# Conditioning blocks moved between the quarters of x, first recurrent block summed chunk by chunk, and a reciprocal root by exp and ln

## What is computed

```python
ada = (silu(c) @ w_ada + b_ada)                 # 6 vectors of 2048: shift1, scale1, gate1, shift2, scale2, gate2
h = rmsnorm(x, g_pre1) * (1.0 + scale1) + shift1
z = h @ w_in                                    # columns: pool | LRU | pool gate | LRU gate
y_pool = pool_mix(u_pool)                       # trailing means, per-group map
xc = causal_dwconv(u_lru)                       # width 4
r, i = sigmoid(xc @ w_rg + b_rg), sigmoid(xc @ w_ig + b_ig)     # 8 diagonal blocks of 256
a = exp(-8 * r * softplus(-lam)); u = sqrt(1 - a**2) * (i * xc)
h_t = a_t * h_{t-1} + u_t                       # the recurrence
x = x + gate1 * rmsnorm((sigmoid(g_pool) * up(y_pool) + sigmoid(g_lru) * up(y_lru)) @ w_out, g_post1)
x = x + gate2 * rmsnorm(conv_ffn(rmsnorm(x, g_pre2) * (1 + scale2) + shift2), g_post2)
```

## Time and profile before

| | |
|---|---|
| median of 3 runs | 2651.7 us (2651.51 to 2810.54) |
| the profiled execution, its own time | 2655.3 us |
| its span on the slowest core | 2653.8 us (cores: 2639.4 to 2653.8) |
| PE busy | 2256.0 us (85%) |
| DVE busy | 1186.9 us (45%) |
| ACT busy | 851.8 us (32%) |
| POOL busy | 146.6 us (6%) |
| mean granted TensorE clock of that core | 0.933 |
| mean DMA rate | 128 GB/s |

### The profile page before, as it was taken

The page is one execution under the profiler, slowest core; times in us unless marked ns, Lnnn a source line. Parts: engine busy times, 40 slices in busy tenths (PEclk is TensorE's granted clock), DMA queues, the critical chain, the costliest instruction groups (busy, mean ns, idle before and its releaser), DMA issues.

```text
span 2653.8 us, 42396 instructions; the slowest of 8 cores (2639.4 to 2653.8 us)
## 1 busy us (share of the span) xinstructions
PE 2256.0 (85%) x16896; PEld 1147.8 (43%) x16896; DVE 1186.9 (45%) x2346; ACT 851.8 (32%) x1111; POOL 146.6 (6%) x281
## 2 busy tenths in 40 slices
PE   2215888887899999997688888999999999999993
PEld 0012444443455555553344444445554545555551
DVE  1842787996511111122445555643003775663005
ACT  2142787885200000011233344432002434442000
POOL 0000000000000000000000000000000000000000
PEclk9557999998899999998898999999999999999996
DMA  9485755464243544466658877778776997778961
GB/s 247 133 134 89 139 108 99 91 116 93 48 88 73 102 89 80 80 120 131 165 96 164 176 138 135 133 143 168 133 130 116 198 186 136 135 135 159 200 126 72
DMA packets 61970, 338.45 MB, mean 128 GB/s; under 512 B 7504, under 2 KB 8016, under 8 KB 28240
## 3 DMA queue, kind: packets, MB, share of 16 engines
q0 software_dynamic: 39888, 273.17, 57.4%
q1 hardware_dynamic: 21888, 62.56, 7.1%
HBM read 586.69 MB, written 22.17 MB: 229 GB/s over the span
## 4 chain that ended last, share of the span: by engine, by line
PE 66%; DVE 11%; DMA 9%; ACT 8%; issue 5%; DVEq 0%; SPq 0%; ACTq 0%; another core or an unknown queue 0%; POOL 0%; POOLq 0%
PE ps_all L251 66%; ACT sb_R L228 6%; DVE sb_R L231 4%; DVE sb_R L234 4%; DMA sb_w<-w_ada 3%; DMA sb_w<-w_ffn_up 2%; DMA sb_R<-xp 2%; DMA sb_R<-x1s 1%; ACT L228 1%; DVE sb_stl L234 1%; DVE sb_rstd L452 1%; DMA sb_w<-w_in 1%; DVE sb_rstd L901 0%; ACT sb_stl L228 0%; DVE sb_wsm L231 0%
## 5 line engine op out<-in xcount | busy, mean ns | idle before, releaser
L251 PE MATMUL ps_all<-sb_R,sb_w 128*128 128x512 bf16 (+4 forms) x14592 | 2076.5, 303 | 76.4 <-ACT sb_R L228 40.4
L251 PEld LDWEIGHTS ps_all<-sb_R,sb_w 128*128 128x128 bf16 x14592 | 1047.0, 98 | 1092.9 <-issue 140.4
L228 ACT ACTIVATE sb_R<-ps_all 128x450 f32<-128x450 f32 (+7 forms) x456 | 254.3, 587 | 1264.1 <-PE ps_all L251 1202.3
L234 DVE SCALAR_TENSOR_TENSOR sb_R<-sb_R,sb_cvec 128x450 f32<-128x450 f32 (+3 forms) x576 | 379.4, 706 | 57.7 <-ACT sb_R L228 45.8
L228 ACT ACTIVATE sb_R<-sb_R 128x577 f32<-128x577 f32 (+8 forms) x200 | 193.7, 972 | 248.4 <-DVE sb_R L248 91.6
L231 DVE TENSOR_TENSOR sb_R<-sb_R 128x128 f32<-128x128 f32 (+9 forms) x148 | 158.9, 1078 | 230.5 <-ACT sb_R L228 172.3
L231 DVE TENSOR_TENSOR sb_wsm<-sb_R 128x577 bf16<-128x577 f32 (+1 forms) x64 | 48.8, 763 | 447.2 <-ACT sb_R L228 445.2
L228 ACT ACTIVATE sb_R<-ps_all,sb_cvec 128x577 f32<-128x577 f32 (+4 forms) x184 | 170.2, 925 | 27.6 <-DVE sb_R L231 15.9
L251 PE MATMUL ps_all<-sb_R,sb_ones 128*128 128x512 bf16 (+3 forms) x144 | 43.2, 419 | 125.9 <-DVE sb_R L231 64.6
L241 DVE TENSOR_SCALAR sb_mod<-ps_all,sb_cvec 128x17 f32<-128x17 f32 x96 | 18.1, 230 | 252.3 <-PE ps_all L251 251.9
L251 PE MATMUL ps_all<-sb_sl,sb_w 128*128 128x17 bf16 x1536 | 46.5, 172 | 89.9 <-DMA sb_w<-w_ada 46.9
(11 more groups left out here) (58 smaller groups left out, 665.9 us busy)
## 6 DMA issues: line engine op xcount, KB each, us to landing
sb_w<-w_ffn_up POOLq DMA_DIRECT2D x96, 1024.0 KB, 10.3
sb_w<-w_ada POOLq DMA_DIRECT2D x48, 1024.0 KB, 10.8
sb_w<-w_ffn_down POOLq DMA_DIRECT2D x48, 1024.0 KB, 9.3
sb_w<-w_in POOLq DMA_DIRECT2D x36, 1024.0 KB, 13.8
sb_w<-w_out POOLq DMA_DIRECT2D x16, 1024.0 KB, 9.7
sb_R<-xm SPq DMA_DIRECT2D x4, 2312.0 KB, 67.0
sb_R<-xp SPq DMA_DIRECT2D x4, 2048.0 KB, 45.2
sb_w<-w_lru_up POOLq DMA_DIRECT2D x8, 1024.0 KB, 7.8
```

The lines of the kernel that those rows point to most:

```text
L228: return self.P.op("act", lambda e: e.activation(out=out, in_=in_, func=func, **kw), after)
L234: return self.P.op("dve", lambda e: e.scalar_tensor_tensor(out=out, in0=in0, scalar=scalar, in1=in1, op0=op0, op1=op1), after)
L251: return self.P.op("pe", lambda e: e.matmul(out, lhsT=lhsT, rhs=rhs, start=start, stop=stop), after, signal)
```

## The change

`front` is rewritten. All squares are on ACT. The conditioning blocks 0 and 1 stand between the quarters of `xp`, blocks 2 and 3 between those of `xm`, blocks 4 to 7 after them; all use one PSUM bank (7) and rotate through three of the four weight slots. The fourth holds the weights of recurrent unit 0 from the start, and `z0(i)` adds the contributions of chunks 2i and 2i+1 to unit 0's sums as soon as `hp` of these is there. S1A(0) keeps only the copies out of PSUM. `h_main` for the last ten chunks of `hm` is recorded behind S1A(0), in the new `front_end`, and the load of `w_pool_grp`, which waits for what ACT and DVE have been given till then, behind that. Root and reciprocal become `Ln` and `Exp(-0.5 ...)` on ACT (`rsqrt`), here and in `rstd_of`. The load of `invc` is issued last on SP. In `S1A`, `wload` now stands behind `wsm_load`, for all units.

```diff
+    def rsqrt(self, r, b, nb, n, after):
+
+        t = self.A(r, self.ap_ps(b, n), AF.Ln, scale=1.0 / D, bias=EPS, after=after)
+        self.release(b, nb, [t])
+        return self.A(r, r, AF.Exp, scale=-0.5, after=[t])
...
+        def ada_pair(i):
+            self.ada_item(1, i, 7)
+            fin[i] = self.ada_item(0, i, 7)
+            if i == 0:
+                z0w.append(self.wload(self.w_in, 4, fixed=3))
...
+        squares(3, *M_)
+        tr = self.rsqrt(self.rstd[:, 0:N], 4, 3, N, [last["m"], t_np[DK - 1]])
+        ada_pair(4)
+        z0(3)
+        h_prev(4)
+        normed(range(0, 6), xm, N, tr, t_nm)
+        ada_pair(5)
+        z0(4)
+        h_prev(5)
+        h_main(0)
+        normed(range(6, 11), xm, N, tr, t_nm)
+        ada_pair(6)
+        z0(5)
+        h_prev(6)
+        h_main(1)
+        h_main(2)
+        normed(range(11, DK), xm, N, tr, t_nm)
+        ada_pair(7)
+        z0(6)
+        h_prev(7)
+        z0(7)
...
+        self.h_left = lambda: [h_main(i) for i in range(3, 8)]
...
             d = info[i]
-            wsl, wt, wi = self.wload(self.w_in, 4 + blk)
             wg, wgt, wgi = self.wsm_load(blk)
...
+            if i == 0:
+                jobs = self.z0_jobs
+            else:
+                wsl, wt, wi = self.wload(self.w_in, 4 + blk)
...
         S1A(0)
+        self.front_end()
+        self.t_wgrp = self.ld(wgrp, self.w_grp, "wgrp", after=self.t_front, eng="pool")
         S1B(0)
         S1A(1)
...
-            ta = self.A(r, self.ap_ps(b, n), AF.Sqrt, scale=1.0 / D, bias=EPS, after=[tok, prior])
-            self.release(b, 2, [ta])
-            return P.op("dve", lambda e: e.reciprocal(out=r, in_=r), [ta])
+            return self.rsqrt(r, b, 2, n, [tok, prior])
```

More of the change, by code:

```diff
@@ L435, in front @@
         sq_free = [None, None]
[L437 to L455, removed]
-            return t
-        t_np = stats(xp, NP, t_xp, 0, 2, [(0, 512), (512, NP)])
-        t_nm = stats(xm, N, t_xm, 2, 3, [(0, 512), (512, 1024), (1024, N)])
         hp = self.bfv(O_HP, 16, SP_)
@@ new lines, in front, with squares @@
+        gM = [(0, 512), (512, 1024), (1024, N)]
+        last = {}
+        t_np, t_nm = [None] * DK, [None] * DK
+        self.t_hp, self.t_hm = [None] * DK, [None] * DK
+        def squares(q, name, xv, n, t_x, b, nb, groups):
+            for k in range(4 * q, 4 * q + 4):
+                s = k % 2
+                tq = self.A(sq[s][:, 0:n], xv[:, k, 0:n], AF.Square, after=[t_x[q], sq_free[s]])
+                for gi, (c0, c1) in enumerate(groups):
+                    d = [tq, t_one] + (self.bfree(b, nb) if k == 0 and gi == 0 else [])
+                    last[name] = self.MM(self.ap_ps(b, c1 - c0, c0), self.ones[:], sq[s][:, c0:c1], k == 0,
+                                         k == DK - 1, d, gi == len(groups) - 1)
+                sq_free[s] = last[name]
@@ L485, in front, with z0 @@
[L485 to L486 removed]
+                self.t_hm[k] = [ta, t2, tz]
+        z0b = [0, 2]
+        def z0(i):
+            w, wt, wi = z0w[0]
+            for k in (2 * i, 2 * i + 1):
+                for c in range(2):
+                    for gi, (c0, c1) in enumerate(gP):
+                        d = [wt] + self.t_hp[k] + (self.bfree(z0b[c], 2) if k == 0 and gi == 0 else [])
+                        t = self.MM(self.ap_ps(z0b[c], c1 - c0, c0), w[:, k, c * 128:(c + 1) * 128], hp[:, k, c0:c1],
+                                    k == 0, k == DK - 1, d, k == DK - 1 and gi == 1)
+                if k == DK - 1:
+                    self.w_rel[wi] = t
@@ new lines, in front @@
+        P_ = ("p", xp, NP, t_xp, 4, 2, gP)
+        M_ = ("m", xm, N, t_xm, 4, 3, gM)
+        squares(0, *P_)
+        ada_pair(0)
+        squares(1, *P_)
+        squares(2, *P_)
+        ada_pair(1)
+        squares(3, *P_)
+        tr = self.rsqrt(self.rstd[:, 0:NP], 4, 2, NP, [last["p"], self.t_sl])
+        normed(range(DK), xp, NP, tr, t_np)
+        h_prev(0)
+        h_prev(1)
+        squares(0, *M_)
+        ada_pair(2)
+        z0(0)
+        z0(1)
+        h_prev(2)
+        squares(1, *M_)
```

87 lines of the change are left out of this document (50 added, 37 removed).

## The result

The changed kernel is slower. Its ratio to the kernel before is **1.041, with a 95% interval of 1.039 to 1.043**, or some 109 us.

What follows compares the result with a forecast made beforehand. TensorE holds 66% of the chain, so time is lost mostly where it stands still. 2655.3 - 36.5 (opening) + 168.6 (recurrent stage) - 5 (root) = 2782.4, with the median at 2779 us, 4.8% above before; range 2735 to 2815.

Steps and rivals of the forecast that it cites:

- z0's end: Opening: the last two chunks of hp and their eight matmuls end at 177 us, paced by VectorE's one queue.
- From there to unit 1: Opening: ScalarE's copies and hm chunks until 194.1, then w_pool_grp, wsm and w_in loads; unit 1 starts at 210.0 us.
- S1A(1) and P1(0): Opening's end: S1A(1) takes 13.95 us plus 2.3 for low clock, P1(0) 5.95, ending at 232.2 us.
- The wait per unit: Recurrent units 2 to 15: TensorE waits 10.7 us for each w_in load behind the wsm load, 14 times.
- The clock: Recurrent units 2 to 15: idle TensorE loses clock, costing 2.1 us more per unit, 14 times.
- What is given back: Recurrent stage: w_in matmuls' 4.4 us of waits for ScalarE and 6.2 us for conditioning weights are saved.
- The whole stage: Recurrent stage: waits and clock of 179.2 us less the savings cost 168.6 us; bounds 93 and 251.
- The root in ffn: Behind the stage: an ACT pass replaces six 3.77 us VectorE reciprocals, 5 us off; bounds 2 and 6.
- The units absorb part of the wait: Rival, recurrent stage: P1's 1.40 us waits for ScalarE vanish, 20 us less, 2759 us; chance 0.15.
- The opening gives nothing: Rival, opening: moved hm chunks, blocked POOL queue and VectorE's queue use up the gain, 2815 us; chance 0.12.
- the clock stays low: Rival, recurrent stage: the clock stays low through each S1A, 180 us more, 2959 us; chance 0.04.
- In time all the same: Rival, recurrent stage: w_in arrives in time despite its place, so not slower, 2610 us; chance 0.05.

Runs made afterwards that it cites:

- experiment 6: experiment 4 with w_pool_grp's load behind unit 3's weights and the last five xm multiplications behind the last conditioning block; 0.974 of before, 2580.9 to 2583.8 us.
- experiment 1: The changed kernel with the w_in load ahead of the gate matrices' (wsm) load again; 0.984 of before, 2608.8 us at the lowest.
- experiment 3: experiment 1 with Sqrt on ScalarE and reciprocal on VectorE again instead of Ln and Exp; 0.988 of before, 2619 to 2626 us.
- experiment 4: experiment 1 with w_pool_grp's load behind unit 1's weights and S1B(0) ahead of front_end; 0.980 of before, 2597.6 us at the lowest.

## Why the prediction was right, and where its sizes were off

The mechanism and the sign held: a load without a reason to wait was put behind one that waits, and TensorE stands still behind it in 14 units. The forecast was 2779 us for the median and 2782.4 for the profiled execution, which took 2767.7. The stage's cost was put 20.0 us too high; the gains of the opening and of the rest were put 2.2 and 3.1 too high, which takes 5.3 of that back. Step by step:

- **z0's end: 177 predicted, 182.1 measured** (176.33 + 5.81). The second half of block 7 waited 10.04 us for VectorE, as the one-queue reading said, but until 175.1 instead of 173, and the matmuls behind it took 5.8 us: `z0(6)` stands behind block 7 as well as `z0(7)`, so they are 16 (15 in the record), where the forecast counted eight. The prediction's bound of 165 for the last weight was not to be had either: in experiment 6 TensorE, no longer held by VectorE, still waited for that weight until 170.8.
- **From there to unit 1: 33.0 predicted, 30.25 measured.** ScalarE's share was right: POOL issued `w_pool_grp` at 198.63, 16.5 us behind z0's end (17.1). From that issue to the first matmul it took 13.8 us, not 15.9. The wsm load ahead of `w_in` thus added nothing to the 14.7 of before.
- **S1A(1) and P1(0): 22.2 predicted, 22.0 measured.** Together the opening gives 34.3 us where 36.5 was forecast. Two misses of 5 and 3 us cancel in part.
- **The wait per unit: 14 x 10.7 = 149.8 predicted, 144.5 measured** (10.3 each). POOL's 0.56 and 0.52 us stood as read, but for the one 0.89. The landing took 8.2 us where the row of `w_ada` in that place had 9.3; the three longer waits gave 9 us back. Cores 1, 5 and 7, without them, waited 134 to 135 us. By the Trainium skill, "DMA: Bandwidth & Descriptors", section "Anatomy of one DMA — SWDGE (gpsimd) path", the landing comes 8.0 us behind the first issue (an estimate from its 2.0 us and 436 GB/s); measured from there it is 0.52 + 8.2 = 8.7, between that and the 9.8 I took.
- **The clock: 14 x 2.1 = 29.4 predicted, 25.8 measured.** S1A takes 16.1 us in the mean of the six P units instead of 13.95, and 17.57 in the eight M units instead of 15.93. Two units of the kernel before had some of this already (15.08 us in the row at 337.88, 17.34 in the one at 402.08, 2.5 us together), which the forecast did not see; they are part of the next term.
- **What is given back: 10.6 predicted, 21.7 measured.** This is the mis-sized term. The groups of TensorE from 234.45 to 730.9 us in the changed kernel:

```profile
L251 PE MATMUL ps_all<-sb_R,sb_w 128*128 128x512 bf16 (+2 forms) x1129 | 235.7, 371 | 145.9 <-DMA sb_w<-w_in 115.2 <-ACT sb_R L228 29.3 <-issue 0.2
L251 PE MATMUL ps_all<-sb_R,sb_wsm 128*128 128x512 bf16 (+2 forms) x289 | 62.8, 357 | 39.2 <-ACT sb_R L228 27.2 <-DVE sb_stl L245 11.1 <-issue 0.4
L251 PE MATMUL ps_all<-sb_sl,sb_w 128*128 128x17 bf16 x544 | 16.0, 171 | 0.0
```

The 6.2 us of waits for conditioning weights and the 4.4 for ScalarE are gone, as said. But P1's matmuls, which the forecast left as they were, also take less. The same group in the kernel before:

```profile
L251 PE MATMUL ps_all<-sb_R,sb_wsm 128*128 128x512 bf16 (+2 forms) x304 | 75.2, 397 | 37.1 <-ACT sb_R L228 25.9 <-DVE sb_stl L245 11.1
```

Busy and idle together it is 102.0 us now against 112.3, 10.3 less, with 357 ns for a matmul instead of 397 (over all cores 357 to 367 instead of 376 to 397). The kernel before lost clock in P1 by itself; one of its rows, and the same twelve matmuls one unit later:

```profile
449.67 3.65 PE L251 MATMUL ps_all<-sb_R,sb_wsm 128*128 128x512 bf16 x12 [1.39 <-ACT sb_R L228]
...
474.32 2.26 PE L251 MATMUL ps_all<-sb_R,sb_wsm 128*128 128x512 bf16 x12 [1.39 <-ACT sb_R L228]
```

The granted clock was 0.56 from 449.60 to 453.20 and 1.00 from 474.30 to 476.60. The forecast priced the clock that S1A loses behind an idle, but not that P1 would lose less of it. (15 matmul records of this group are missing in the trace of after. They are also missing in that of experiment 1, where the group has 71.1 us busy and 40.9 idle, 112.0, so they don't explain the 10.) The four parts, 6.2, 4.4, 10.3 and 2.5, make 23.4, somewhat over the 21.7, since rows overlap at their ends. Why P1 keeps its clock better behind the stalls is open.
- **The whole stage: 168.6 predicted, 148.6 measured**: 5.3 too much for the waits, 3.6 for the clock, 11.1 too little given back.
- **The root in ffn: 5 us predicted, not resolved.** The rest of the program got 1.9 us shorter in the profiled pair and 6.0 in the mean of all cores, and experiment 3 shows 3 us at the end and no more that could be told from scatter. The Trainium skill, "ScalarE: Activation LUTs", section "Table sets: the hidden batching unit", has ln and exp in one set; the trace agrees, with no load between the rows at 2727.33 and 2728.08.
- **The rivals.** "The units absorb part of the wait" gave 2759 by a mechanism that isn't there: P1's last group still waits for ScalarE, 0.91 us in units 1 and 2 and 1.38 to 1.61 in most others. That the measured time is nearer to its 2759 than to the forecast is chance. "The opening gives nothing" and "the clock stays low" fell with the rows at 212.39 and 345.53. "In time all the same" asked for under 3.7 us of wait and clock together; its number, 2610, is that of experiment 1 (2609 to 2614 us), which is the changed kernel without the exchange.

## What to carry to other kernels

A queue that issues in program order makes every load behind a waiting one wait too. When two loads are exchanged, write down for each which instruction frees its target, and put the one that is free first ahead; here that one line decided between 0.984 and 1.041. After a gain in one place look at the next load that stands behind a waiting one: experiment 4 won 31 us in the opening and kept some 10, and some 11 more came only when that next load was freed. And when a stall is priced with the clock it costs, read also where the kernel loses clock without it.
